# Moving one small transpose of each attention head one step later, next to another one

## The reference, cut to what matters

```python
proj = x @ w_in
q, k, v, f_logit = jnp.split(proj, [D_MODEL, 2 * D_MODEL, 3 * D_MODEL], axis=-1)
...
for qb in range(S // Q):                      # 8 blocks of 128 queries
    logits = jnp.einsum('bqhd,bkhd->bhqk', q[:, t0:t1], k[:, :t1]) * scale
    logits = logits + c[:, :, t0:t1, None] - c[:, :, None, :t1]
    p = jax.nn.softmax(jnp.where(causal, logits, -jnp.inf), axis=-1)
    outs.append(jnp.einsum('bhqk,bkhd->bqhd', p, v[:, :t1]))
o = jnp.concatenate(outs, axis=1).reshape(B_, S, D_MODEL)
return o @ w_out
```

## Time and profile before

| | us |
|---|---|
| median of three executions | 1648.62 (1647.34 to 1650.56) |
| the profiled execution, its own time | 1649.76 |
| its span, first to last instruction | 1648.1 |
| PE busy | 1581.8 (96%) |
| DVE busy | 1188.4 (72%) |
| ACT busy | 1031.4 (63%) |

### The profile page before, as it was taken

How to read it: one execution, slowest core, us unless ns; L and a number is a source line. 1 busy time by engine, 2 the same in 40 slices (tenths; PEclk the granted TensorE clock), 3 DMA queues, 4 the chain that set the end, 5 groups by cost and what they waited for, 6 DMA issues and landing times.

```text
span 1648.1 us, 32180 instructions
## 1 busy us (share of the span) xinstructions
PE 1581.8 (96%) x8246; PEld 1313.5 (80%) x8247; DVE 1188.4 (72%) x2036; ACT 1031.4 (63%) x1705; POOL 515.5 (31%) x495
## 2 busy tenths in 40 slices
PE   6999999999999999899999999999999999999985
PEld 6897888888887788778888888788888888888863
DVE  4214777777777887846777787767876787888857
ACT  3214666666666654526677787666776777877854
POOL 0000000000000134532554464543454454454526
PEclk9999999999999999899999999999999999999995
DMA  7223322222223534557999999999999999999986
GB/s 244 90 81 90 72 52 64 59 63 70 52 64 113 177 116 160 202 190 277 329 300 319 300 357 367 329 288 267 336 316 284 280 354 324 347 368 365 375 258 250
DMA packets 161319, 368.63 MB, mean 224 GB/s; under 512 B 53008, under 2 KB 73488, under 8 KB 161264
## 3 DMA queue, kind: packets, MB, share of 16 engines
q1 hardware_dynamic: 136272, 284.21, 49.4%
q0 software_dynamic: 24992, 83.73, 19.7%
HBM read 294.39 MB, written 65.11 MB: 218 GB/s over the span
## 4 chain that ended last, share of the span: by engine, by line
PE 72%; DVE 7%; issue 7%; DMA 5%; ACT 4%; ACTq 1%; POOL 1%; another core or an unknown queue 1%; POOLq 1%; DVEq 1%; SPq 0%
PE bank L1023 6%; PE bank L1026 6%; PE bank L1029 6%; DMA sums_scratch<-ys,sidx 4%; PE q_ps L91 4%; PE q_ps L93 4%; PE q_ps L92 4%; PE out_ps L914 4%; PE k_ps L893 3%; PE out_ps L1082 3%; PE out_ps L1083 3%; PE q_ps L1013 3%; PE k_ps L1050 2%; PE k_ps L1051 2%; PE k_ps L1058 2%
## 5 line engine op out<-in xcount | busy, mean ns | idle before, releaser
L1915 DVE TENSOR_TENSOR gu_lo<-raw_gu,gu_hi 128x1024 fp32r<-128x1024 f32 x260 | 306.4, 1220 | 25.7 <-ACT gu_hi L1394 23.3
L1394 ACT CAST gu_hi<-raw_gu 128x1024 fp32r<-128x1024 f32 x260 | 253.3, 1050 | 1.2 <-DMA raw_gu<-in_moe_w_up_dram 1.2
L1023 PE MATMUL bank<-gu_hi,xb_hi 128*128 128x512 f32 x576 | 234.5, 407 | 6.3 <-DVE gu_lo L1915 3.2
L1026 PE MATMUL bank<-gu_lo,xb_hi 128*128 128x512 f32 x576 | 228.1, 396 | 0.0
L681 POOL DMA_INDIRECT sums_scratch<-ys,sidx x63 | 124.3, 1973 | 144.7 <-DMA sums_scratch<-ys,sidx 108.7
L1915 DVE TENSOR_TENSOR dn_lo<-raw_dn,dn_hi 128x1024 fp32r<-128x1024 f32 x130 | 152.7, 1213 | 2.4 <-ACT dn_hi L1394 1.8
L1029 PE MATMUL bank<-gu_hi,xb_lo 128*128 128x512 f32 x576 | 142.5, 389 | 0.0
L1023 PEld LDWEIGHTS bank<-gu_hi,xb_hi 128*128 128x128 f32 x576 | 110.9, 193 | 29.9 <-issue 7.3
L612 POOL IOTA e<- 128x64 f32 x1 | 0.2, 185 | 429.0 <-DVE xs L1711 429.0
L1299 ACT CAST pt_hi<-k_ps 128x512 fp32r<-128x512 f32 (+1 forms) x192 | 85.8, 482 | 75.4 <-PE k_ps L893 74.7
L1394 ACT CAST dn_hi<-raw_dn 128x1024 fp32r<-128x1024 f32 x130 | 130.0, 1052 | 2.3 <-DMA raw_dn<-in_moe_w_down_dram 2.3
(11 more groups left out here) (305 smaller groups left out, 3991.5 us busy)
## 6 DMA issues: line engine op xcount, KB each, us to landing
raw_gu<-in_moe_w_gate_dram SPq DMA_DIRECT2D x128, 512.0 KB
raw_gu<-in_moe_w_up_dram SPq DMA_DIRECT2D x128, 512.0 KB
raw_dn<-in_moe_w_down_dram SPq DMA_DIRECT2D x128, 512.0 KB
wqk<-in_fox_w_in_dram SPq DMA_DIRECT2D x66, 128.0 KB, 2.5
v_scratch<-v_out SPq DMA_DIRECT2D x32, 256.0 KB, 2.8
va<-v_scratch SPq DMA_DIRECT2D x16, 512.0 KB, 4.8
fin<-sums_scratch SPq DMA_DIRECT2D x16, 512.0 KB, 9.6
xs<-in_x_dram SPq DMA_DIRECT2D x8, 512.0 KB, 8.3
```

Of the source, the lines that this page charges most:

```text
L1023: i = pe.matmul(o3, xb_hi[s][:, c], g_hi[:, :, c], start=c == 0, stop=False, skip_group_check=True)
L1026: pe.matmul(o3, xb_hi[s][:, c], g_lo[:, :, c], start=False, stop=False, skip_group_check=True)
L1394: a.copy(hi, raw).then_inc(S[done], 1)
L1915: dve.tensor_tensor(lo, raw, hi, ALU.subtract).then_inc(S[lo_ok], 1)
```

## The change

Turn 6 moves from step 3 to step 4, where turn 7 already stands. PE, ACT and DVE all read the list, so the transpose, its high half and its low half move together. No instruction is added or removed.

```diff
-STEP_TURNS = [(0, 1), (2, 3), (4, 5), (6,), (7,), (8, 9), (10, 11), (12, 13)]
+STEP_TURNS = [(0, 1), (2, 3), (4, 5), (), (6, 7), (8, 9), (10, 11), (12, 13)]
```

## The result

| | before | after |
|---|---|---|
| median of 20 executions, us | 1647.32 (1641.96 to 1650.56) | 1649.32 (1646.30 to 1653.26) |
| ratio, 95% interval | | 1.0015 [1.0008, 1.0022] |
| span of the profiled execution, us | 1648.1 | 1647.8 |

The change makes the kernel slower by 0.15%, that is 2.5 us (1.3 to 3.6 us). It is clear of zero and a little under the forecast of 3.4 us. The forecast of the time itself, 1652.0 us, is 2.7 us above the measured 1649.32: 1.3 us of that is the start of the sum, the median of three executions (1648.62) where 20 give 1647.32. The spans of the two profiled executions say nothing of it (0.3 us the other way): single executions of either kernel spread over 7 to 9 us. A change of 3 us has to be read inside the trace, in the stretch that it touches.

The account below looks back on a forecast made before the run. Heads 1 to 14 looked like pure PE work, but the weighing in step 3 waits for DVE's `added`. 14 x 0.22 + 0.34 = 3.4 us on the median 1648.62 gives 1652.0 us, range 1648.6 to 1653.8.

Parts of the forecast that it names:

- Turn 6 stands in a hole: Step 3: PE waits for DVE's `added` there anyway, so taking the turn out starts the weighing no earlier; gain nothing.
- 0.22 us a head in step 4: PE in step 4: five blocks take 0.47 us instead of 0.25, with no hole there; 14 heads cost 3.1 us.
- The slack at slot 7 is no slack: Even heads: PE's wait at slot 7 saves nothing, as DVE's maxima carry the full 0.22 us to the next head.
- absorption: Rival: six even loop heads absorb the cost at slot 7, leaving 0.07 us each; 2.5 us in all, 1651.1; chance 18%.
- The halves hidden in 14 heads, 0.34 us in head 15: ACT's and DVE's halves fit into idle time in step 4; only head 15, bound by DVE, pays 0.34 us.
- Head 0 costs nothing: Head 0 has no weighing; PE's step 4 ends in a 2.20 us wait for slot 4's exponential: cost 0.
- The sum: Whole kernel: 14 x 0.22 + 0.34 = 3.4 us, put on the median 1648.62, gives 1652.0 us.
- the clock's play: Last head: where the stretch at 1.2 GHz falls can change, by up to 1.7 us of PE time either way.
- The unknown of the other distance from `added`: Step 3: each head's 0.05 or 0.15 us from `added` to the weighing may switch, -0.8 to +0.6 us in all.
- The rival on the other side: Step 3: PE's own switch from turn to weighing, not `added`, holds the weighing; 1.2 us faster, 1647.4; chance 10%.

## Why the prediction was right

- **"Turn 6 stands in a hole": right.** This was the step on which all hung. Doubling the turn in place cost 0.33 us over 14 heads (0.5 forecast), the distances from L1704 to the weighing stayed at 0.15 and 0.06 us after the change in all 14, and with the sum and the low half of turn 4 early, the hole was gone and the two blocks took 0.14 us.
- **"0.22 us a head in step 4": right**, by itself (3.11 / 14) and in the change (3.05 / 14 = 0.218). A block costs 0.11 us of PE's stream here. The Trainium skill, "TensorE: Matmul & The Clock Gate", has about 81 ns for a pair of weight load and matmul at 128 columns in "Back-to-back issue gap" and about 275 ns in "PE-mode transpose"; as estimates from these the 28 blocks would have cost 2.3 or 7.7 us. The 3.11 us of the run lie between, and the modelled duration of 0.275 us is not what a block takes from the others.
- **"The slack at slot 7 is no slack": right.** 3.05 and 3.11 us, not the 2.2 that these heads would have cost with absorption. Head 6 is 0.10 us longer and the head ahead of it 0.30. This fits the chain over DVE's maxima, ACT's exponentials and `turned_low`, which hands the delay on to the next head's first turn: the odd heads pay it. The chain itself was read from rows; no run broke it at one link.
- **The halves hidden in 14 heads, 0.34 us in head 15: right** (0.03 and 0.31 us with the halves alone, tail 0.30 us in the change).
- **Head 0 costs nothing: right**, at equal clock. From its first mask matmul to that of head 1 it took 22.17 us with turn 6 in step 3 and 22.16 to 22.17 in step 4 where no stretch at 1.2 GHz fell, and 23.7 us in either where one fell.
- **The sum:** 3.05 + 0.30 = 3.35 us where the trace can be read, for 3.4 forecast. The timed ratio says 2.5 us with an interval of 1.3 to 3.6, which holds it. Where the 0.9 us between the two lie stays open, if they are more than noise. The stretch behind the attention differs by more than that between the two profiles (1087.7 us before, 1084.7 after). The higher mean clock of the executions with turn 6 in step 4 would work in this direction; the prediction had the clock's play among its unknowns for the last head alone, and no term for it elsewhere. The unknown of the other distance from `added` (-0.8 to +0.6 us) did not come true; both distances stayed.
- **The rival on the other side** needed the weighing to start before the sum ends. It did not. But the experiment with the sum alone ahead showed a state of the same kernel in which the very same change gains 5.2 us, which I had not listed.

## What to carry to other kernels

When work moves out of a place, look first at what the next instruction there starts on. If that is another engine's result, the work that leaves only lengthens a wait, and it costs its full price where it goes, even though the engine's busy share says it is always busy. Read the starts, not the durations: two blocks that take 0.37 us in one place and 0.14 us in another show a hidden wait of 0.23 us. And a slack that one engine shows behind the new place is worth nothing when another engine's chain started ahead of it.

## What the runs showed of the hardware

- Where it waited for L1704, the first weighing matmul kept a fixed distance to the end of that DVE instruction: 0.05 to 0.06 us in the even loop heads and 0.15 us in the others, to 0.01 us over 14 heads, before and after the change. The trace shows a difference that goes with it: in the even loop heads the weight load itself carries the wait for `added`, in the others a semaphore instruction of its own stands ahead of the load, 0.11 us before the matmul. No run changed this alone, so that it is the cause is not shown.
- The stretch at 1.2 GHz behind a wait of 2.0 to 2.2 us on PE in head 0 came in 8 of 12 profiled executions, with turn 6 in either step, and cost 1.6 us each time. The split of the first nine profiles looked like a rule and was none; whether the change makes the stretch rarer is open.
